# Two merging layers and one output layer of a three-block model, from single fp32 products to three rounded ones

## The reference, cut to what matters

```
# second block (512-wide branches y_a, y_b; w_o is 1024 x 1024)
m = jax.nn.sigmoid(gate_a) * (y_a @ w_a) + jax.nn.sigmoid(gate_b) * (y_b @ w_b)
return x + rms_norm_2(m @ w_o, norm_post)
...
# third block (three 256-wide branches)
ya = (ya * jax.nn.gelu(lru_gate)) @ w_out_lru[l]
yb = (jax.nn.sigmoid(m_o) * from_heads(hb)) @ w_out_mlstm[l]
yc = from_heads(hc) @ w_out_sb[l]
merged = (jax.nn.sigmoid(g_a) * ya + jax.nn.sigmoid(g_b) * yb
          + jax.nn.sigmoid(g_c) * yc)
x = x + merged @ w_o[l]
# then a feed-forward layer on the normalized x
```

## Time and profile before

| what | us |
|---|---|
| median of 3 runs | 2018.55 |
| lowest and highest run | 2016.25, 2020.31 |
| time of the profiled execution | 2018.23 |
| its span, first to last instruction | 2016.5 |
| PE busy within the span | 1975.5 |
| DVE, ACT, POOL busy | 1496.9, 1187.1, 58.2 |

### The profile page before, as it was taken

The page is one execution under the profiler, slowest core; times in us unless marked ns, Lnnn a source line. Parts: engine busy times, 40 slices in busy tenths (PEclk is TensorE's granted clock), DMA queues, the critical chain, the costliest instruction groups (busy, mean ns, idle before and its releaser), DMA issues.

```text
span 2016.5 us, 31654 instructions
## 1 busy us (share of the span) xinstructions
PE 1975.5 (98%) x12242; PEld 1740.3 (86%) x12242; DVE 1496.9 (74%) x1628; ACT 1187.1 (59%) x1269; POOL 58.2 (3%) x105
## 2 busy tenths in 40 slices
PE   8999999999999999999999999999999999999997
PEld 7699998688888888888888888889988899989997
DVE  7776554889999999899999999986585368446652
ACT  5164443778777787777778777773354365325442
POOL 3020000000000000000000000010000000030000
PEclk9999999999999999999999999999999999999999
DMA  7535453499999999999999999974522334444551
GB/s 254 172 126 178 178 191 123 153 366 374 357 371 360 366 373 356 371 364 364 364 367 372 359 373 363 365 295 159 197 85 105 125 128 145 168 151 184 189 185 45
DMA packets 75863, 510.23 MB, mean 253 GB/s; under 512 B 8320, under 2 KB 14464, under 8 KB 14592
## 3 DMA queue, kind: packets, MB, share of 16 engines
q1 hardware_dynamic: 75776, 508.98, 67.7%
HBM read 506.66 MB, written 2.29 MB: 252 GB/s over the span
## 4 chain that ended last, share of the span: by engine, by line
PE 89%; DVE 5%; issue 2%; ACT 2%; DMA 1%; POOL 0%; ACTq 0%; DVEq 0%; SPq 0%; POOLq 0%
PE ps L921 9%; PE ps L925 9%; PE ps L924 9%; PE ps L653 9%; PE ps L656 8%; PE ps L657 8%; PE ps L946 5%; PE ps L950 5%; PE ps L949 5%; PE ps L630 3%; PE ps L1221 2%; PE ps L1224 2%; PE ps L1223 2%; PE ps L1147 1%; PE ps L932 1%
## 5 line engine op out<-in xcount | busy, mean ns | idle before, releaser
L1945 DVE TENSOR_TENSOR ring_r<-ring,high 128x2048 fp32r<-128x2048 f32 x227 | 517.7, 2290 | 53.1 <-ACT high L1602 31.7
L1602 ACT ACTIVATE high<-ring 128x2048 fp32r<-128x2048 f32 x224 | 428.5, 1914 | 14.8 <-DMA ring<-w_stream 14.4
L1818 DVE TENSOR_TENSOR ring_r<-ring,high 128x2048 fp32r<-128x2048 f32 x115 | 263.3, 2293 | 123.8 <-ACT high L1405 123.6
L924 PE MATMUL ps<-ring_r,big_r 128*128 128x512 f32 x896 | 349.6, 390 | 0.0
L656 PE MATMUL ps<-scr_r,high 128*128 128x256 f32 (+1 forms) x1200 | 343.1, 286 | 0.0
L1405 ACT ACTIVATE high<-ring 128x2048 fp32r<-128x2048 f32 x115 | 218.7, 1908 | 161.4 <-PE ps L653 92.3
L1945 DVE TENSOR_TENSOR ring_r<-ring,scr_r 128x2048 fp32r<-128x2048 f32 x112 | 256.5, 2290 | 39.6 <-ACT scr_r L1602 39.0
L653 PE MATMUL ps<-sq_r,high 128*128 128x272 f32 (+1 forms) x832 | 238.6, 287 | 5.6 <-DVE scr_r L1836 5.6
L657 PE MATMUL ps<-sq_r,ring_r 128*128 128x272 f32 (+1 forms) x832 | 238.1, 286 | 0.0
L656 PEld LDWEIGHTS ps<-scr_r,high 128*128 128x128 f32 x1200 | 227.4, 189 | 0.2
L1602 ACT ACTIVATE scr_r<-ring 128x2048 fp32r<-128x2048 f32 x112 | 214.5, 1915 | 20.0 <-DMA ring<-w_stream 19.8
(11 more groups left out here) (485 smaller groups left out, 3800.9 us busy)
## 6 DMA issues: line engine op xcount, KB each, us to landing
ring<-w_stream SPq DMA_DIRECT2D x477, 1024.0 KB, 4.8
big<-spread SPq DMA_DIRECT2D x32, 146.0 KB, 3.0
spread<-big SPq DMA_DIRECT2D x8, 151.0 KB, 4.9
h<-h_in SPq DMA_DIRECT2D x1, 1088.0 KB, 5.1
out<-hn SPq DMA_DIRECT2D x1, 1024.0 KB, 4.7
vec<-vec_in SPq DMA_DIRECT2D x1, 576.0 KB, 8.2
```

The lines of the kernel that those rows point to most:

```text
L924: pe.matmul(o, x_item_high[:, k, :], w_low[:, cols], start=False, stop=False)
L1602: act.activation(w_high, w, ACT.Copy).then_inc(S["moe_high"], 1)
L1818: dve.tensor_tensor(w_low, blocks_at(c, 0, CH), w_high.bitcast(F32), ALU.subtract).then_inc(S["weights_low"], 1)
L1945: dve.tensor_tensor(w_low, w, w_high.bitcast(F32), ALU.subtract).then_inc(S["moe_low"], 1)
```

## The change

The stages `w_o2`, `outs3` and `w_o3` are put into `SPLIT_STAGES`, and PE multiplies there in three rounded products. `pair` goes. For that ACT and DVE make high and low parts of 4, 3 and 4 chunks more, and of the activations: ACT copies each merged tile (`merged_high2`, `merged_high3`), DVE subtracts (`low_part` for tile m-2 behind the multiplications of tile m, and for the last two at the end). `y3`, the input of `outs3`, is split in one instruction each. The chunks of `w_o2` are split between the tiles; of `w_o3` DVE splits one chunk behind tile 1 and three behind the last tile, ACT one before the first tile, one behind tile 4, two behind tile 7. `outs3` uses banks 3 to 5 for even tiles and 0 to 2 for odd ones; `w_o3` starts at bank 4 instead of 0.

```
-SPLIT_STAGES = ("pw1", "pw2", "ffn0_in", "ffn0_out", "w_in2a", "w_in2b0", "w_in2b", "w_in3", "ffn3_in", "ffn3_out")
+SPLIT_STAGES = ("pw1", "pw2", "ffn0_in", "ffn0_out", "w_in2a", "w_in2b0", "w_in2b", "w_o2", "w_in3", "outs3", "w_o3",
+                "ffn3_in", "ffn3_out")
...
+        def out3_bank(half, br):
+            return (3, 0)[half] + br
+        def wo3_bank(j):
+            return 2 * ((2 * j + 2) % 3)
...
# PE, w_o2 (w_o3 in the same way, with merged_high3 and wo3_bank(j))
-                pair(BOFF["w_o2"] + j * KD, KD, lambda k: hn256[:, k, :], SEQ, b, S["wo2_done"],
-                     (lambda k: pe.wait_ge(S["br_ready"], k + 1)) if j == 0 else None)
+                split_pair(BOFF["w_o2"] + j * KD, KD, merged_high2, hn_r, SEQ, b, S["wo2_done"],
+                           after_split("w_o2") if j == 0 else None)
...
# PE, outs3
+            pe.wait_ge(S["input_low"], LOWS["outs3"] + 1)
...
+                            mm = pe.matmul(o, w_high[:, cols], y3_high[:, 2 * br + k, :], start=(k == 0), stop=False)
...
+                            pe.matmul(o, w_high[:, cols], y3_low[:, 2 * br + k, :], start=False, stop=False)
+                            mm = pe.matmul(o, w_low[:, cols], y3_high[:, 2 * br + k, :], start=False, stop=(k == 1))
...
# ACT
+            split_weights(BOFF["w_o2"] // CH)
+            for m in range(KD):
+                act.wait_ge(S["br_ready"], m + 1)
+                act.activation(merged_high2[:, m, :], hn256[:, m, :], ACT.Copy).then_inc(S["input_high"], 1)
+                if m % 2:
+                    split_weights(BOFF["w_o2"] // CH + min((m + 1) // 2, 3))
...
+            split_weights(BOFF["w_o3"] // CH)
+            for m in range(KD):
+                act.wait_ge(S["merged"], m + 1)
+                act.activation(merged_high3[:, m, :], hn256[:, m, :], ACT.Copy).then_inc(S["input_high"], 1)
+                if m in (4, 7):
+                    split_weights(BOFF["w_o3"] // CH + (1, 3)[(4, 7).index(m)])
...
# DVE
+                if m >= 2:
+                    low_part(hn_r[:, m - 2, 0:SEQ], hn256[:, m - 2, :], merged_high2[:, m - 2, :], "input_low")
+                if m in (1, 3, 5):
+                    split_weights(BOFF["w_o2"] // CH + (1, 3, 5).index(m))
...
+                if m >= 2:
+                    low_part(hn_r[:, m - 2, 0:SEQ], hn256[:, m - 2, :], merged_high3[:, m - 2, :], "input_low")
+                if m == 1:
+                    split_weights(BOFF["w_o3"] // CH)
+            for m in (KD - 2, KD - 1):
+                low_part(hn_r[:, m, 0:SEQ], hn256[:, m, :], merged_high3[:, m, :], "input_low")
+            split_weights(BOFF["w_o3"] // CH + 3)
```

More of the change, by code:

```diff
@@ L101 @@
 assert len(MOE_ORDER) == MOE_CH
-SPLIT_STAGES = ("pw1", "pw2", "ffn0_in", "ffn0_out", "w_in2a", "w_in2b0", "w_in2b", "w_in3", "ffn3_in", "ffn3_out")
+SPLIT_STAGES = ("pw1", "pw2", "ffn0_in", "ffn0_out", "w_in2a", "w_in2b0", "w_in2b", "w_o2", "w_in3", "outs3", "w_o3",
+                "ffn3_in", "ffn3_out")
 SPLIT_ALL = [c for _name, _n in STAGES if _name in SPLIT_STAGES
              for c in range(BOFF[_name] // CH, (BOFF[_name] + _n) // CH)]
+LOWS = {}
+LOWS_N = 0
+for _name, _n in (("pw1", KD), ("pw2", KD), ("ffn0", KD), ("w_in2", KD), ("w_o2", KD), ("w_in3", KD), ("outs3", 1),
+                  ("w_o3", KD), ("ffn3", KD)):
+    LOWS[_name] = LOWS_N
+    LOWS_N += _n
 CARRIED = list(range(C_POST, C_POST + LOOK))
@@ L619, in begun @@
                     mm.then_inc(pre_begun if at_chunk[0] < C_MOE else post_begun, 2 if at_chunk[0] == C_POOL + 1 else 1)
[L621 to L635, removed]
             def split_pair(b0, kt, x_high, x_low, t, bank, done, inputs=None):
@@ L1207, in half_pair @@
                     if p == 0 and half == 0:
-                        pe.wait_ge(S["input_low"], 8 * 4 + k + 1)
+                        pe.wait_ge(S["input_low"], LOWS["w_in3"] + k + 1)
                     if half == 0:
@@ L1350, in _ @@
                     for br in range(3):
-                        if j == 0 and 3 * half + br in bank_owner:
-                            claim(3 * half + br)
+                        if j == 0 and out3_bank(half, br) in bank_owner:
+                            claim(out3_bank(half, br))
                         for k in range(2):
                             b = BOFF["outs3"] + j * 6 + 2 * br + k
[L1355 to L1359, removed]
+                            if half == 0:
+                                w_high, w_low, first = parts_of(b)
+                                if first:
+                                    begins.append(b)
+                            else:
+                                w_high, w_low = parts_at(b // CH, b % CH, b % CH + 1)
+                            cols = slice(half * P, half * P + P)
+                            o = ps[:, out3_bank(half, br), 0:SEQ]
+                            mm = pe.matmul(o, w_high[:, cols], y3_high[:, 2 * br + k, :], start=(k == 0), stop=False)
                             if half and b in begins:
                                 mm.then_inc(post_begun, 1)
+                            pe.matmul(o, w_high[:, cols], y3_low[:, 2 * br + k, :], start=False, stop=False)
+                            mm = pe.matmul(o, w_low[:, cols], y3_high[:, 2 * br + k, :], start=False, stop=(k == 1))
                     mm.then_inc(S["out3_done"], 1)
             for j in range(4):
-                b = 2 * (j % 3)
+                b = wo3_bank(j)
                 if j == 0:
@@ L1368, in _ @@
                     pe.wait_ge(S["merged"], 8)
-                pair(BOFF["w_o3"] + j * KD, KD, lambda k: hn256[:, k, :], SEQ, b, S["wo3_done"],
-                     (lambda k: pe.wait_ge(S["merged"], k + 1)) if j == 0 else None)
+                split_pair(BOFF["w_o3"] + j * KD, KD, merged_high3, hn_r, SEQ, b, S["wo3_done"],
+                           after_split("w_o3") if j == 0 else None)
                 bank_owner[b] = (S["x3_ready"], 2 * j + 1)
                 bank_owner[b + 1] = (S["x3_ready"], 2 * j + 2)
-            ffn(1, 9, 5, SEQ, in_low, hid_high, hid_low, BOFF["ffn3_in"], BOFF["ffn3_out"],
+            ffn(1, 9, "ffn3", SEQ, in_low, hid_high, hid_low, BOFF["ffn3_in"], BOFF["ffn3_out"],
                 lambda j, k: None, lambda j: sum_tiles(10, SEQ, range(4)) if j == 2 else None)
@@ L1777, in _ @@
                        .then_inc(S["fl_ready"], 1)
+                if p == 16:
+                    act.wait_ge(S["lru_in"], 1)
+                    act.wait_ge(S["sb_y"], 1)
+                    act.wait_ge(S["mh_ready"], 1)
+                    act.activation(y3_high, y3, ACT.Copy).then_inc(S["input_high"], 1)
                 if p >= 15:
@@ L2303, in _ @@
                 ins.then_inc(S["br_part"], 1)
+                if m >= 2:
[3 more added lines that the diff above has]
+            for m in (KD - 2, KD - 1):
+                low_part(hn_r[:, m, 0:SEQ], hn256[:, m, :], merged_high2[:, m, :], "input_low")
+            split_weights(BOFF["w_o2"] // CH + 3)
             split_weights(BOFF["w_in3"] // CH + 2)
@@ L2450, in _ @@
                        .then_inc(S["lru_in"], 1)
+                if p == 17:
+                    low_part(y3_low, y3, y3_high, "input_low")
                 if p == 13:
```

19 lines of the change are left out of this document (12 added, 7 removed).

## The result

The changed kernel takes **2006.64 us** (median of 5 runs, 2004.65 to 2007.40), the kernel before took 2016.98 on the same chip (5 runs, 2016.25 to 2020.31). The ratio of the two on record is **0.9936, 95% interval 0.9921 to 0.9950**: 0.64% faster. The two medians divided give 0.9949, at the upper end of that interval. The forecast was 2007.3, with a range of 2003 to 2012.

A forecast was written before the change was run, and what follows sets the result against it. PE, busy 1975.5 of 2016.5 us, was taken as the bound. Terms -13.60 - 1.15 + 0.19 + 1.2 + 0.5 + 1.1 + 0.5 = -11.3 took 2018.23 to 2006.95, median 2007.3; range 2003 to 2012.

The forecast's parts named there:

- PE is the bound, so the products carry the gain: `w_o2`, `outs3`, `w_o3`: three rounded matmuls at 0.118 us replace each fp32 product, gains 4.99, 3.81, 4.80, together 13.60 us.
- fourth rival: In the newly rounded stages weight loads aren't hidden, 0.19 us a matmul, so the kernel is slower, 2042 us; chance 3%.
- The banks, -1.15: Start of `outs3`: beginning in banks 3 to 5 removes PE's wait for bank 0, 1.15 us less.
- Changes of format, +0.19: Where PE goes from fp32 to rounded products, the second matmul comes 0.19 us later; net +0.19 over `w_o2` and `ffn3_in`.
- The wait at the fifth branch, +1.2: Second block's merge: DVE's chunk split holds up POOL's addition of tile 1, so PE waits 1.2 us before the fifth branch.
- Inside `outs3`, +0.5: Third block: the split of `w_o3`'s first chunk delays tile 2's multiplications; PE waits 0.5 us for the bank before tile 4.
- second rival: In `outs3` low parts and additions wait for each other, a tile costs 2.6 us instead of 2.12; 2011.6 us, chance 15%.
- The second chunk of `w_o3`, +1.1: After E (PE's end of the last `outs3` tile), DVE splits that chunk until E + 6.8; PE waits 1.1 us.
- first rival: POOL isn't held up by DVE: fifth branch and chain behind `outs3` lose 1.2 and 0.5 us of waits; 2005.5 us, chance 20%.
- DVE behind time, +0.5: Third block: two more splits make DVE late, so PE waits 0.5 us for tile 6's low part in the first `ffn3_in` pair.
- third rival: Waits and a spell of low granted clock eat the gain, 2015 to 2018 us, within 0.2%; chance 5%.
- No other price in groups of two: In `outs3`, rounded matmuls in groups of two products cost the same as in groups of eight, 0.118 us each.

The follow-up runs named there:

- experiment 4: Kernel before with only the other bank order (`outs3` in banks 3 to 5 first, `w_o3` from bank 4), products still fp32; one run, 2018.87 us.
- Experiment 1: Kernel before plus one two-input VectorE subtract, 128x2048, behind the multiplications of tile 1 at the second block's merge; single time 2017.92 us.
- experiment 3: Changed kernel with VectorE's first `w_o2` chunk split behind tile 2 instead of tile 1; 2006.22 us, ratio to the kernel before 0.9950.
- experiment 2: Kernel before plus one one-input VectorE maximum over 128x2048, behind the multiplications of tile 1 at the second block's merge; single time 2027.26 us.

## Why the prediction was right, step by step

**PE is the bound, so the products carry the gain: right.** Rounded matmuls stand 0.118 to 0.120 us apart in all three stages, and the stages lose nearly what the sum gave them (table at the end of this section). The fourth rival (weight loads set the pace, 2042) is out: it had 0.19 a matmul, and a loss from 0.143 on.

**The banks, -1.15: right**, and shown alone in experiment 4 (0.13 us instead of 1.27).

**Changes of format, +0.19: wrong, it costs nothing.** Behind fp32 matmuls the first rounded one is recorded 0.18 us early, on top of the last: the eight sums of squares seem to take 1592.34 to 1593.88 = 1.54 us where they took 1.72 before. The second then stands 0.31 behind, 0.19 more than the usual 0.12. The two cancel. For the same reason `w_o3` before took 27.44 + 0.18 = 27.62 us, like `w_o2`, and not 27.44. This is read from the records only; no run was made for it. At the start of `ffn3_in` the term came out (-0.18, by which `w_o3` had looked too short); the two of +0.19 at `w_o2` did not exist, so the sum was 0.38 too high.

**The wait at the fifth branch, +1.2: right in mechanism and size.** POOL's pair, VectorE's split, PE:

```profile
1557.82 3.46 POOL L2634 TENSOR_TENSOR hn<-scr 128x256 f32<-128x256 f32 x2 [197.16 <-DVE scr L2329]
```
```profile
1558.32 2.37 DVE L1846 TENSOR_TENSOR ring_r<-ring,high 128x2048 fp32r<-128x2048 f32 x1
```

The split ends at 1560.69, the addition 0.59 later, and PE starts at 1561.33, where without a wait it would have been 1553.23 + 6.94 = 1560.17: 1.16 us. Experiment 1 makes the same wait without any rounded product, experiment 3 takes it away by moving one instruction. The Trainium skill (SBUF — State Buffer, Who interferes with whom) has the rule: a VectorE instruction with two SBUF inputs contends with a GpSimd instruction that reads SBUF, and one with at most one SBUF input, outside its 2-port modes, doesn't. The trace agrees with the first half, 3.46 us for the pair instead of 1.41, and experiment 2 with the second, 1.41.

**Inside `outs3`, +0.5: right place, half the size.** PE and VectorE there:

```profile
1765.86 0.28 PE L1371 MATMUL ps<-big_r,ring_r 128*128 128x256 f32 x1
1766.20 0.39 PE L1367 MATMUL ps<-big_r,high 128*128 128x256 f32 x1
```
```profile
1765.06 1.08 DVE L2513 TENSOR_TENSOR scr<-ps,big 128x256 f32<-128x256 f32 x3
```

PE ends the fourth tile with a matmul at 1765.86 and begins the next at 1766.20, 0.22 more than the usual 0.12. VectorE's multiplications of tile 2 ran from 1765.06 to 1766.14, which is 8.79 us after the start of `outs3` (I had 8.95), and PE wanted them at 1765.98, which is 8.63 (I had 8.49), since the matmuls stand 0.120 apart here and not 0.118. The hand-over takes 0.06.

**DVE and POOL pace `outs3` (second rival): the mechanism exists, the price doesn't.** Low parts wait for additions and additions for low parts. First VectorE, behind tiles 2 and 3 and then behind tile 5, then POOL:

```profile
1766.06 0.77 DVE L1864 TENSOR_TENSOR hn_r<-hn,h_r 128x256 fp32r<-128x256 f32 x1
1766.76 1.07 DVE L2513 TENSOR_TENSOR scr<-ps,big 128x256 f32<-128x256 f32 x3
1767.75 0.78 DVE L1864 TENSOR_TENSOR hn_r<-hn,h_r 128x256 fp32r<-128x256 f32 x1
1768.65 1.09 DVE L2513 TENSOR_TENSOR scr<-ps,big 128x256 f32<-128x256 f32 x3
...
1770.81 1.09 DVE L2513 TENSOR_TENSOR scr<-ps,big 128x256 f32<-128x256 f32 x3 [0.57 <-PE ps L1371]
1771.81 0.41 DVE L1864 TENSOR_TENSOR hn_r<-hn,h_r 128x256 fp32r<-128x256 f32 x1
```
```profile
1763.03 2.72 POOL L2638 TENSOR_TENSOR scr<-scr 128x256 f32<-128x256 f32 x1 [0.55 <-DVE scr L2513]
1765.82 0.73 POOL L2639 TENSOR_TENSOR hn<-scr 128x256 f32<-128x256 f32 x1
1766.51 0.92 POOL L2638 TENSOR_TENSOR scr<-scr 128x256 f32<-128x256 f32 x1
```

A low part takes 0.77 or 0.78 where POOL is adding and 0.41 where it isn't. But a tile's turn while they catch up is 1768.65 - 1766.76 = 1.89 us, below PE's 2.12: VectorE gains on PE, and from 1770.81 on it is VectorE that waits. The rival summed both hold-ups for each tile; they fall together, because the one that waits does so while the other works.

**The second chunk of `w_o3`, +1.1: right place, 0.4 too much.** PE waits from 1780.62 to 1781.28, 0.66 us. I had the last low part end at E + 4.5, it ended at E + 4.0:

```profile
1776.13 1.29 DVE L1864 TENSOR_TENSOR hn_r<-hn,h_r 128x256 fp32r<-128x256 f32 x2
1778.51 0.43 DVE L1864 TENSOR_TENSOR hn_r<-hn,h_r 128x256 fp32r<-128x256 f32 x1 [1.09 <-ACT h_r L1806]
1778.85 6.69 DVE L1846 TENSOR_TENSOR ring_r<-ring,high 128x2048 fp32r<-128x2048 f32 x3
```
```profile
1776.29 0.85 POOL L2638 TENSOR_TENSOR scr<-scr 128x256 f32<-128x256 f32 x1 [0.50 <-DVE scr L2513]
```

I let POOL's addition wait for both low parts. It asked during the first (1776.29) and got in between the two, in 0.85 us instead of some 1.3, and the second low part waited for it. ACT's copy took 0.42, not the 0.51 that I had taken from a copy with a scale. So the hold-up that I had charged here hardly exists: the prediction's own chain without it, 6.23 and a wait of 0.6, is what came. At this place the first rival had the better price.

**DVE behind time, +0.5: nearly nothing.** VectorE reached tile 2 at E + 11.97 and tile 6 at E + 26.27, 14.30 later (I had 12.45 and 14.4); the half microsecond is the one from the step above. PE waits 0.04: 0.16 us from 1801.90 to 1802.06, less the usual 0.12. It waits for the low part of tile 5, which ends at 1802.00, and not for that of tile 6, as I had it. So that term of the sum was the previous one counted on.

**Together.** By stage, predicted against measured:

| stage | predicted | measured |
|---|---|---|
| second merge (-4.99 + 0.38 + 1.2) | -3.4 | -3.66 |
| banks | -1.15 | -1.13 |
| `outs3` (-3.81 + 0.5) | -3.3 | -3.21 |
| `w_o3` (-4.80 + 1.1) | -3.7 | -3.91 |
| first `ffn3_in` pair (+0.5 - 0.19) | +0.3 | -0.05 |
| sum | -11.3 | -11.96 |

The waits cost 1.16 + 0.22 + 0.66 + 0.04 = 2.1 us, where I had 3.3, and the format change nothing at `w_o2`, where I had 0.38: 1.6 us too pessimistic. Of that 0.9 went again: the stages without their waits are longer than the sum's 0.118 a matmul makes them, `outs3` by 17.58 - 0.22 - 16.98 = 0.38, `w_o3` by 23.53 - 0.66 - 22.64 = 0.23, the rest 0.3 in `w_o2` and `ffn3_in`. Part of it belongs to the waits: behind each of the three in the third block a second matmul comes late as well, at a distance of 0.22, 0.20 and 0.22 us (1766.20 to 1766.42, 1781.28 to 1781.48, 1802.06 to 1802.28) instead of 0.12, together 0.28. The largest other part is in `outs3`: with groups of two products the distance averages 0.120 instead of 0.118, about 0.3 us over 144 matmuls. "No other price in groups of two" was nearly right, not quite. Why isn't known. No clock spell fell into the merges (granted clock 1.00 from 1541 to 1620 and from 1757 to 1798 us), so the third rival's condition wasn't met.

**How much of it was luck.** The median is 0.7 us from the forecast, and that is closer than the working deserves. The errors named above, 1.6 and 0.9, went against each other. And the forecast had set out from 2018.23, where the median before is 2016.98: the medians lie 10.3 us apart, the spans of the two traces 13.7, and the runs of either kernel spread over 3 to 4 us. What the record supports is the stage table, an error of 0.7 in 11.96, and not the last digit of the time.

## What to carry to other kernels

Where PE sets the end, count its matmul starts and then every other engine's queue instruction by instruction; a helper's work costs only where someone is queued behind it. Here a single weight split that stood one tile too early cost as much (1.16 us) as the whole bank wait (1.15). Where VectorE and GpSimd work on the same stage, treat a VectorE instruction with two inputs in SBUF and a GpSimd addition as shutting each other out, and put the long ones where the other has nothing due; making them shorter and more frequent didn't help here. Before moving a split, look at who makes its input: the engine that does may have it last in its own queue.

## What the runs showed of the hardware

**The exclusion works in both directions.** The prediction said that no row showed VectorE waiting for a running addition. The rows chosen for it didn't, but the trace of the kernel before has such a place: POOL begins an addition of 1.30 us (128x512) at 140.13, VectorE a chunk split at 140.59, and the split takes 2.98 us instead of 2.29. The new rows agree: a split begun during an addition takes 2.82 us instead of 2.29 (experiment 3, 1563.24), a low part 0.77 instead of 0.41, while an addition under a split takes up to 2.72 instead of 0.72.

**Whoever asked first gets the next turn.** POOL's addition at 1776.29 asked while a low part ran and went ahead of VectorE's next low part, though that one stood right behind. In experiment 3 its addition at 1563.08 asked during a low part (1562.91 to 1563.32) and went ahead of the split of 1563.24. The other way round, at 1558.32 in the changed kernel, the split came before the addition of tile 1, since POOL was still at that of tile 0. So several short two-input instructions in a row let POOL in after the first, where one long one keeps it out to its end. In the additions that meet no long instruction but a low part just before, the cost is small: 0.84 instead of 0.72.

**A one-input instruction that reads as much is harmless**: 2.27 us of VectorE over POOL's pair, which took its 1.41. It wrote only 128x1.

**Start times across a change of number format can't be taken at face value**: the first rounded matmul behind fp32 ones is recorded 0.18 us early and with 0.47 instead of 0.28 us, and the next one 0.31 instead of 0.12 behind it.
